# FFN second half as seven half-size products, with f stored by tile, the gate applied from PSUM and GpSimd adding token blocks in three products

## What is computed

```python
def _conv_ffn(h, w_gu, conv_w, conv_b, w_down):
    ...
    return (jax.nn.silu(gc) * u) @ w_down
...
    h = _norm(x) * (1 + scale2) + shift2
    x = _affine_ln(ALPHA * x + gate2 * _conv_ffn(h, w_gu, conv_w, conv_b, w_down), ln2_g, ln2_b)
```

## Time and profile before

| | |
|---|---|
| median of 3 runs | 2961.4 us (2961.13 to 2963.22) |
| the profiled execution: its own time, its span | 2957.74 us, 2955.9 us |
| `ffn_up_phase`, `ffn_down_phase` in the span | some 964 us to 2373.7, then 582 us |
| TensorE, VectorE, ScalarE, GpSimd busy over the span | 92%, 60%, 42%, 16% |

### The profile page before, as it was taken

One profiled execution on the slowest core, in us unless ns is written; L12 is line 12 of the kernel. 1 busy time (PEld: TensorE's weight loads), 2 busy tenths in 40 slices (PEclk: granted clock), 3 DMA queues, 4 the chain that ended last, 5 costly groups with the idle time before them and its releaser, 6 DMA issues. The chain is left out here.

```text
span 2955.9 us, 50052 instructions
## 1 busy us (share of the span) xinstructions
PE 2725.3 (92%) x17011; PEld 2475.6 (84%) x17011; DVE 1769.5 (60%) x3030; ACT 1232.2 (42%) x2612; POOL 471.0 (16%) x678
## 2 busy tenths in 40 slices
PE   4999999676999978996999999999999979999996
PEld 4999999565888866885999999999999968888875
DVE  4534332346999974777887876667666534352445
ACT  2211111115988971234555565556555522112121
POOL 0000000124444431223001000000000000230312
PEclk8999999887999998997999999999999989999999
DMA  8223222498675814563655564444444354334233
GB/s 290 82 92 120 79 92 64 169 358 176 137 153 118 162 50 149 185 197 86 226 176 170 166 205 151 151 153 149 151 151 155 107 173 139 107 128 139 85 126 130
DMA packets 400709, 435.71 MB, mean 147 GB/s; under 512 B 122592, under 2 KB 293654, under 8 KB 397848
## 3 DMA queue, kind: packets, MB, share of 16 engines
q1 hardware_dynamic: 377216, 414.28, 46.7%
q10 hardware_dynamic: 21016, 11.29, 1.3%
q0 software_dynamic: 2304, 7.88, 0.8%
HBM read 311.18 MB, written 124.57 MB: 147 GB/s over the span
## 5 line engine op out<-in xcount | busy, mean ns | idle before, releaser
L2202 PE MATMUL fu_alpha<-fu_h,fu_w 128*128 128x384 f32 x3168 | 576.3, 336 | 17.8 <-DVE fu_h L2428 10.6
L2688 PE MATMUL fd_acc<-fd_w,fd_f 128*128 128x512 f32 x2376 | 546.7, 392 | 28.5 <-DVE fd_w L2716 19.1
L2202 PEld LDWEIGHTS fu_alpha<-fu_h,fu_w 128*128 128x128 f32 x3168 | 555.1, 189 | 20.4 <-issue 20.3
L2688 PEld LDWEIGHTS fd_acc<-fd_w,fd_f 128*128 128x128 f32 x2376 | 447.4, 189 | 127.8 <-issue 19.1
L2202 PE MATMUL fu_beta<-fu_h,fu_w 128*128 128x384 f32 x1584 | 287.1, 335 | 0.6 <-DVE fu_h L2428 0.6
L2202 PEld LDWEIGHTS fu_beta<-fu_h,fu_w 128*128 128x128 f32 x1584 | 277.1, 189 | 1.1 <-issue 1.1
L598 PE MATMUL pj_gps<-pj_ht,w_in 128*128 128x256 f32 x2160 | 268.9, 285 | 0.0
L598 PEld LDWEIGHTS pj_gps<-pj_ht,w_in 128*128 128x128 f32 x2160 | 263.5, 191 | 1.3
L2712 DVE TENSOR_TENSOR fd_f<-fd_f_stage,fd_f 128x512 fp32r<-128x512 f32 (+1 forms) x110 | 91.5, 833 | 284.7 <-ACT fd_f L2668 284.7
L2668 ACT CAST fd_f<-fd_f_stage 128x512 fp32r<-128x512 f32 (+1 forms) x110 | 63.5, 579 | 443.5 <-PE fd_acc L2688 395.5
L2402 DVE TENSOR_TENSOR fu_w<-up_w_stage,fu_w 128x512 fp32r<-128x512 f32 x264 | 181.7, 689 | 85.6 <-ACT fu_w L2266 83.6
(11 more groups left out here) (221 smaller groups left out, 4125.6 us busy)
## 6 DMA issues: line engine op xcount, KB each, us to landing
up_w_stage<-in_w_gu_dram SPq DMA_DIRECT2D x88, 512.0 KB, 4.1
fu_w_sums<-w_gu_sums SPq DMA_DIRECT2D x132, 256.0 KB, 3.9
fd_w_stage<-in_w_down_dram SPq DMA_DIRECT2D x54, 512.0 KB, 3.7
fd_f_stage<-f_t SPq DMA_DIRECT2D x88, 256.0 KB, 2.6
at_k<-k_t SPq DMA_DIRECT2D x28, 704.0 KB, 13.0
w_gu_sums<-fu_w_sums SPq DMA_DIRECT2D x66, 256.0 KB, 4.8
fo_w<-in_w_ada_dram SPq DMA_DIRECT2D x8, 2048.0 KB, 18.1
up_w_stage<-in_w_gu_dram SPq DMA_DIRECT2D x44, 256.0 KB, 4.3
```

The costliest lines, as they stand in the source:

```text
L2202: mm = pe.matmul(out, w[x][:, j, k, :], b[y][:, j, k, :], start=opens and (k, x, y) == (0, HI, HI), stop=(k, x, y) == (KH - 1, LO, HI), sk ...
L2688: mm = pe.matmul(acc[:, t, at], f[a][:, slot, t * P:(t + 1) * P], w[b][:, w_at(st, slot), at], start=is_step(st, 0) and (a, b) == (HI, HI) ...
```

## The change

`ffn_down_phase` is written anew as a block algorithm with seven half-size products where eight are usual. Two token tiles (rows 0 and 1), the two halves of the 22 channel blocks and the two halves of the 1024 columns give 2x2 blocks on each side; a product multiplies a sum or difference of two token blocks (`A_OF`) by a sum or difference of two weight blocks (`B_OF`), and is added to or taken from one or two blocks of the result (`SUMS`). The seven products are taken one after another (`ORDER`), each over nine pairs of tiles: 63 units, with 11 channel blocks, three passes and 512 columns, so 33 matmuls in a unit. The result of all 18 tiles stays in SBUF (`res`), where ALPHA * x is put at the start.

Five products need a sum of two token blocks (128x1408 floats, 704 KB): the second block is loaded to `f_more`, which exists once, and added in place to `f_raw`, which exists three times. In products 5, 1 and 2 GpSimd adds (L2940), in 7 and 6 (and for the very first unit) VectorE (L2836). GpSimd also adds the weight blocks (L2933). VectorE multiplies each product by the gate, reading PSUM (L2856), then adds that to the result (L2866). The tails of the even tiles run during product 7, of the odd ones during product 6. `f_t` is stored by token tile, so that a block of 128 tokens and 11 channel blocks is 5632 bytes in one piece per partition. The spans are shifted by one token, so `store` issues one-token, whole-tile and cut-tile DMAs.

```diff
                 def store(n, p, f, par):
...
-                    elif p < SPANS - 1:
-                        sp.dma_start(f_t[rows, t0:t0 + SPAN], res[:, par, 0:SPAN]).then_inc(stored[par], 16)
...
+                    if p:
+                        with nc.allow_non_contiguous_dma(reason="one token of the tile ahead"):
+                            sp.dma_start(f_t[t0 - 1, :, bass.ds(f, 1), last:P].rearrange("p f c -> p (f c)"), res[:, par, 0:1]).then_inc(stored[par], 16)
+                    if p < SPANS - 1:
+                        sp.dma_start(tiles(per_span - 1), of_tiles(c0, per_span - 1)).then_inc(stored[par], 16)
...
+    ORDER = (5, 3, 1, 4, 7, 2, 6)
+    A_OF = {1: ((0, 0), (1, 1), ALU.add), 2: ((1, 0), (1, 1), ALU.add), 3: ((0, 0), None, None), 4: ((1, 1), None, None),
+            5: ((0, 0), (0, 1), ALU.add), 6: ((1, 0), (0, 0), ALU.subtract), 7: ((0, 1), (1, 1), ALU.subtract)}
...
+    PIECES = ((0, 2), (2, 6), (6, KH))
+    AHEAD = 6
+    RING = KH + AHEAD
+    WSLOTS, XSLOTS, HSLOTS, BANKS = 3, 3, 2, 8
...
+        def slices_first(u):
+
+            j, i = divmod(u, PAIRS)
+            return [j * KH + k for k in (KH - 2, KH - 1)] if i == 0 and 0 < j < len(ORDER) else []
...
+            if i == PAIRS - 1:
+                return [(j + 1) * KH + k for k in range(AHEAD, KH - 2)]
+            return [(j + 1) * KH + i - 2] if 2 <= i < 2 + AHEAD else []
...
+                def load_unit(u):
+                    if u >= XSLOTS:
+                        sp.wait_ge(unit_done, u - XSLOTS + 1)
+                    load_f(u)
+                    if sums_f(u) and u:
+                        wait_summed(sp, max(n for n in range(u) if sums_f(n)), 0 if u > 1 else len(PIECES) - 1)
+                        load_more(u, more_staged)
...
+                for u in range(UNITS):
+                    j, i = divmod(u, PAIRS)
+                    if u >= BANKS:
+                        pe.wait_ge(gated, u - BANKS + 1)
...
+                    if u:
+                        gate_product(u - 1)
+                    if u + 1 < UNITS:
+                        low_f(u + 1)
+                    if u:
+                        add_product(u - 1)
+                        statistics(u - 1)
+                    for b in slices(u):
+                        low_w(b)
+                    if u + 2 < UNITS:
+                        sum_f(u + 2)
+                    if has_tail(u - 1):
+                        negative_offset(u - 1)
...
+                def sum_w(b):
+                    if sums_w(b):
+                        s = (b - KH) % WSLOTS
+                        pool.wait_ge(w_staged[s], 16 * w_loads(b))
+                        pool.tensor_tensor(wst[:, s, 0, :], wst[:, s, 0, :], wst[:, s, 1, :], B_OF[ORDER[b // KH]][2]).then_inc(w_summed, 1)
...
+                def sum_f(u):
+                    if slow_sum(u):
+                        s = u % XSLOTS
+                        pool.wait_ge(f_staged[s], 16 * f_loads(u))
+                        pool.wait_ge(more_staged, 16 * (sum_count(u) - len(PIECES)))
+                        pool.tensor_tensor(f_raw[:, s], f_raw[:, s], f_more[:, :, :], A_OF[form(u)][2]).then_inc(f_summed_slow, 1)
...
-    f_t = scratch("f_t", [D_FF, T_ALL])
+    f_t = scratch("f_t", [T_ALL // P, P, FT, P])
```

More of the change, by code:

```diff
@@ L2613, in ffn_down_phase @@
[L2613 to L2626 removed]
+        acc = ps("fd_acc", [P, BANKS, NH])
@@ new lines, in ffn_down_phase, with pieces, f_count, sum_count @@
+        vec = lambda t: LAT if t < T_LAT // P else CTX
+        sums_f = lambda u: A_OF[form(u)][1] is not None
+        sums_w = lambda b: B_OF[ORDER[b // KH]][1] is not None
+        def pieces(u):
+            return PIECES if u == 0 else ((0, KH),)
+        def f_count(u, piece=0):
+            return piece + 1 if u == 0 else len(PIECES) + u
+        def sum_count(u, piece=0):
+            return piece + 1 if u == 0 else len(PIECES) + sum(sums_f(n) for n in range(1, u + 1))
+        def slow_sum(u):
+            return u > 0 and form(u) in (5, 1, 2)
@@ new lines, in wait_summed, with f_loads, w_loads @@
+        def wait_summed(eng, u, piece=0):
+            if slow_sum(u):
+                eng.wait_ge(f_summed_slow, sum(slow_sum(n) for n in range(u + 1)))
+            else:
+                eng.wait_ge(f_summed, sum_count(u, piece) - sum(slow_sum(n) for n in range(u + 1)))
+        def f_loads(u):
+            return sum(n > 0 for n in range(u % XSLOTS, u + 1, XSLOTS))
+        def w_loads(b):
+            return sum(2 if sums_w(n) else 1 for n in range(KH + (b - KH) % WSLOTS, b + 1, WSLOTS))
@@ new lines, in load_w @@
+                def load_w(b):
+                    s = (b - KH) % WSLOTS
+                    if b - KH >= WSLOTS:
+                        sp.wait_ge(w_low, b - WSLOTS + 1)
+                    first, second, _ = B_OF[ORDER[b // KH]]
+                    for at, block_of in enumerate((first, second)):
+                        if block_of is not None:
+                            kh, nh = block_of
+                            sp.dma_start(wst[:, s, at, :], w_blocks[kh, b % KH][:, half(nh)]).then_inc(w_staged[s], 16)
@@ L2675, in _ @@
+                normalise(UNITS - 2)
             @block.tensor
             def _(pe):
[L2677 to L2692 removed]
@@ new lines, in gate_product @@
+                def gate_product(u):
+                    if u == 0:
+                        dve.wait_ge(consts_loaded, 64)
+                    else:
+                        dve.wait_ge(added, add_count(u - 1))
+                    dve.wait_ge(unit_done, u + 1)
+                    c = vec(2 * pair(u))
+                    for n, nh in enumerate(sorted({nh for _, nh, _ in SUMS[form(u)]})):
+                        last = dve.tensor_tensor(tmp[:, n, :], acc[:, u % BANKS, :], gate[:, c, half(nh)], ALU.mult)
+                    last.then_inc(gated, 1)
```

462 lines of the change are left out of this document (272 added, 190 removed).

## The result

The changed kernel takes **3001.7 us** (median of 4 runs, 3000.7 to 3002.8) against 2961.9 for the kernel before beside it: ratio 1.0142, 95% interval 1.0128 to 1.0156, so 40 us slower. The profiled execution took 3000.72 us, its span 2998.8.

What follows compares the result with a forecast made beforehand. TensorE was taken to bound the kernel; 7.1 + 469.2 + 16.5 + 37 + 36 + 36 + 23 + 1 = 625.8 us for the second half, against 582.2, gave 3005 us, range 2960 to 3045.

Steps and rivals of the forecast that it cites:

- the borders: Six changes between products: late weight blocks through three staging slots, 4 us in the first unit and 2 in the next; 36 us.
- the tails: Products 7 and 6: GpSimd's 1024-column rows take turns with VectorE, units of 11.1 us, ten units pay; 36 us (18 to 50).
- The start's "about 26": First unit of the second half: loads and first additions make it end at about 26 us instead of 14.6.
- products 5, 1, 2: Units there take 9.1 us through 8.2 us of non-overlapping work and one f_more, 1.7 over TensorE, 22 units; 37 us.
- first half: First half of the FFN: more store pieces, DMA's share from 0.50 to about 0.7, covered by TensorE; 1 us (0 to 3).
- The mechanism: Second half: a GpSimd addition and a VectorE instruction with two SBUF inputs take turns, each for its whole length.
- Rival A: Second half: turns cost little, shared work averages about 7.5 us a unit, TensorE's lead evens it out; 2913 us, chance 0.13.
- Rival B: Second half: waits come to half the forecast's as tails and borders overlap better; within 6 us of 2961, chance 0.04.
- the 125 us of waits: Sign on TensorE's line in the second half: some 125 us of waits released by VectorE's low parts of f and weights.
- L2841 at 2.2 us or more: Sign in the second half: VectorE's low part of f, 1.62 us undisturbed, has a mean of 2.2 us or more.
- Clock: TensorE after longer waits: granted clock falls, 1.9 us each; covered where the pair sets the pace, elsewhere 0 (up to 8).
- rival C: First half: store pieces delay weight loads, 66 steps pay up to 2.8 us each; slower still, 3065 us, chance 0.05.

Runs made afterwards that it cites:

- e7: The kernel before with only the change's stores of f by token tile, its second half reading the new layout: 2962.5 us against 2959.9.
- e1: The changed kernel with the token sums of products 5, 1 and 2 moved from GpSimd back to VectorE: 2970.7 us.
- e2: The changed kernel with GpSimd adding the token blocks in products 7 and 6 too: 3025.8 us.
- e3: The changed kernel without GpSimd's two 1024-column rows (times ln_g, plus ln_b) in 17 of the 18 tails: 2945.4 us.
- e6: The changed kernel with five staging slots for weight blocks instead of three, and no tiles for ln_g and ln_b: 2971.2 us.
- e8: e5 with three weight blocks' low parts first on VectorE in each product's last unit, and ScalarE scaling x behind the weight casts: 2924.1 us.
- e5: The changed kernel with token sums and the tails' 1024-column rows on VectorE, ScalarE's normalising row and L2885 dropped: 2938.9 us.

## Why the prediction was right, and which terms were mis-sized

It said 3005 us and slower; it was 3001.7. The sum of the terms, 625.8 us for the second half, met 621.7. The single terms are less good than that: the borders came out 21 us over, products 5, 1 and 2 18 under and the tails 7.5 under. That the sum is met to 4 us is luck; that it is slower, and why, is not. The start's "about 26" is not covered by the parts that the prediction names, which add up to 23.3; the first unit ended at 26.0 all the same.

| term | predicted | measured in the changed kernel |
|---|---|---|
| first matmul | 7.1 | 7.5 |
| matmuls, 63 units | 469.2 | 471.2 (63 x 7.48) |
| start | 16.5 (6 to 22) | 16.7: units of 18.5, 11.4, 9.2 |
| products 5, 1, 2 | 37 (0 to 57) | 19: 9 in 5, 0 in 1, 10 in 2 |
| tails | 36 (18 to 50) | 28.5: 16.4 in 7, 12.1 in 6 |
| six borders | 36 (12 to 54) | 57: 12.3, 11.2, 8.3, 2.6, 13.2, 9.3 |
| end | 23 (16 to 27) | 21.8 |
| first half | 1 (0 to 3) | 0 to 5 (e7) |

**The mechanism is right.** Moving GpSimd's additions away gives 29 us (e1), adding them to two more products costs 26 (e2), leaving the tail rows out gives 54 (e3, with their work gone and not moved). Rival A failed on this: VectorE was busy for 445 of 592 us, rows that stood in turns included, so there was room by load, but not in time. Its "averages only about 7.5 us a unit" was also miscounted: it left out the five weight blocks at each border, and with all eleven of a product the prediction's own prices give 8.6. Rival B asked for half of the 125 us of waits; the terms came to 121. The rule of the Trainium skill (SBUF — State Buffer, SBUF: two separate sides) is that a VectorE instruction with two SBUF inputs and a GpSimd instruction that reads SBUF block each other whole, whichever starts first; the trace agrees, down to the 128x1 row that took 2.35 us beside a GpSimd row of 2.40.

**Products 5, 1, 2: "1.7 us over TensorE, for 22 units".** In product 2 the round is 8.7 us and the unit with it, as worked out (the prediction took 9.1). In product 1 every one of the seven units took 7.48. The step that failed is counting all 22 units. GpSimd's additions there started 8.4, 9.4 and 8.8 us apart at first, but the late border had let them run ahead: the token sum of the second unit was finished 12.1 us before its unit began, that of the sixth 4.2. From then on they came every 7.4 to 7.6 us. Load and addition are 4.3 and 3.2 there and 4.4 and 4.2 in product 2: the 0.8 us for which VectorE holds up an addition, in the prediction's every round, was 0 in the one and 1.0 in the other, by what VectorE had under way when the addition began. The sum of 8.2 us that can't overlap was no bound either: the same list of rows passed in 7.5. In product 1 the wait at the border (11.2 us) covered the wait behind it; in product 2 both were paid (13.2 and 10). The sum of the two terms was 73 and came out at 76.

**Borders: "4 us late in the first unit and 2 in the next".** The term is 57 against 36, over its upper bound of 54. The second units are late by 1.9 us in the mean, as predicted; the first ones by 7.5. I followed the staging slots and SP's queue and not ScalarE's, where three casts stood 9 us behind the scaling of x at the first border: there the staging slots came free 14.1 us after the last unit's start, where the prediction had a round of 5.2 to 5.8, and the next load took 3.6 where it had 3.2 (the earlier trace rows has 3.7 for 512 KB). For the other five borders no run separates what makes them late. More slots take 27 of the 57 (e6), token additions off GpSimd 9 (e1), and the two moves of e8 34 more than e5, of which some 15 come back in the last units.

**Tails.** The size of the term held in products 7 and 6, but the mechanism reached further than I put it: 14.5 us of product 2 and 12.4 of the end hang on the same rows (e3). What I named as the sign, L2841 at 2.2 us or more, was 1.98, and e1 and e3 show that its excess is the tails' alone; the token additions show in L2866 and L2846. L2940 at 3.60 (over 3.3) and the units of product 7 and 6 (10.4 and 10.7, not 11) were right.

**Clock: "elsewhere I count 0 (up to 8)".** In the changed kernel 110 matmuls follow their predecessor at 0.38 to 0.50 us instead of 0.2257, 17 in the kernel before: 22 us against 3. The granted clock is 0.94 in the matmul stretch (0.99). In the first microseconds after the wait at 2468, when VectorE's low part of f had kept TensorE waiting for 2.48 us, it is 0.63:

```profile
2468.50:2472.50 4.00, 4.00 (x12) 3.15 (x13) 4.00 (x6) 1.77 (x2) 3.48 (x2) 0.63 0.09 18
```

Those 22 us lie within the measured terms of the table; as a term of its own the clock was left out. With TensorE's 98 us of idle time they make 120, and only so does the sign "some 125 us of waits" hold.

**First half, and rival C.** e7's queue has 460,288 packets (377,216), by the stores and the finer reads, for 0 to 5 us. DMA's share in the first half was 0.51 and 0.52, not the predicted 0.7: the mean of 59 ns a packet was no price for these pieces. The Trainium skill (DMA: Bandwidth & Descriptors, Specifications) says that pieces under 512 B are read, modified and written. No run here shows that by itself.

## What to carry over

Before work is moved to GpSimd, add up what VectorE reads twice from SBUF and what GpSimd does in the same unit: these lengths can add, more or less by which engine starts first, and the free time that a busy share shows is not free for them. Here VectorE, with no more than the weight sums and deviations left to GpSimd, did all of it in less time than the two together: the seven products, 40 us slower in the form given, became 44 us faster with token sums and tails on VectorE and a few rows moved at the borders. When waits are summed, ask of each whether the one before it has already built the lead that hides it; here it did in one product and not in another.

## What was not expected of the hardware

A VectorE row with two SBUF inputs pays for GpSimd by GpSimd's length and not by its own: the 128x1 row L2885 has a mean of 2087 ns over 17 instances beside GpSimd's 1024-column rows and 156 ns without them (e3). The same holds the other way: GpSimd's 128x1 L2946 takes 1.46 us when it starts inside a VectorE addition of 1.57, and 0.19 alone. So small steps of a chain (deviation, offset) suffered most here, for their size, from being spread over both engines.
